# Two residual blocks on one core: the gate and the second mixer read their input turned without its norm

## The reference, cut to what matters

```
x = x + mix @ w_out
gate = sigmoid(rms_norm(x, g1) @ w_ple_gate + b);  x = x + gate * e
proj = rmsnorm(x, g2) @ w_in_2
xr, q, ckv, qi, ki, wi, gr, ga = split(proj)
y_rnn = rg_lru(causal_conv(xr), ...)            # 16 blocks of 128 columns
ckv = rmsnorm(ckv, g3);  ki = layernorm(ki)
y_attn = attention(q, ckv, relu(qi . ki) * wi, ...)   # 16 heads
x = x + (sigmoid(gr) * y_rnn + sigmoid(ga) * y_attn) @ w_o
x = x + peer(rmsnorm(x, g4), ...)
rms_norm(x, g) = x * rsqrt(mean(x * x) + eps) * g
```

## Time and profile before

| | |
|---|---|
| runs | 2815.0, 2816.63, 2817.1 us; median 2816.63 |
| profiled execution | 2815.1 us, span 2813.3 us |
| busy: PE, DVE, ACT, POOL | 2759.1, 1811.2, 1391.6, 257.1 us |
| DMA | 183 GB/s over the span |

### The profile page before, as it was taken

One profiled execution on the slowest core, in us unless ns is written; L12 is line 12 of the kernel. 1 busy time (PEld: TensorE's weight loads), 2 busy tenths in 40 slices (PEclk: granted clock), 3 DMA queues, 4 the chain that ended last, 5 costly groups with the idle time before them and its releaser, 6 DMA issues.

```text
span 2813.3 us, 49430 instructions
## 1 busy us (share of the span) xinstructions
PE 2759.1 (98%) x15452; PEld 2411.5 (86%) x15452; DVE 1811.2 (64%) x2894; ACT 1391.6 (49%) x2020; POOL 257.1 (9%) x342
## 2 busy tenths in 40 slices
PE   8999999899999999999999999999999999999998
PEld 6888877788888888889999999888888888888887
DVE  6666655657986666578886666666665555555555
ACT  5454545545565444455555554545554444444444
POOL 0000000000000000000004998000000000000000
PEclk9999999999999999999999999999999999999999
DMA  6544454464554444555565444666665556555574
GB/s 244 191 151 164 162 175 155 165 210 154 167 172 163 157 150 142 186 193 185 183 207 175 159 155 157 216 211 212 209 211 193 194 194 193 191 192 193 193 236 159
DMA packets 153551, 514.71 MB, mean 183 GB/s; under 512 B 17056, under 2 KB 33696, under 8 KB 152480
## 3 DMA queue, kind: packets, MB, share of 16 engines
q1 hardware_dynamic: 131904, 480.44, 52.0%
q10 hardware_dynamic: 21600, 33.70, 3.3%
HBM read 501.49 MB, written 12.58 MB: 183 GB/s over the span
## 4 chain that ended last, share of the span: by engine, by line
PE 59%; DVE 0%; ACT 0%; issue 0%; POOL 0%; DVEq 0%; ACTq 0%; POOLq 0%
PE bank L493 13%; PE bank L2111 8%; PE bank L2113 8%; PE bank L2112 8%; PE bank L498 6%; PE bank L478 3%; PE bank L479 3%; PE bank L480 3%; PE bank L2086 2%; PE bank L533 1%; PE bank L532 1%; PE bank L531 1%; PE bank L2061 0%; DVE act L1086 0%; PE bank L2131 0%
## 5 line engine op out<-in xcount | busy, mean ns | idle before, releaser
L455 DVE TENSOR_TENSOR w_lo<-raw,w_hi 128x1024 fp32r<-128x1024 f32 x904 | 1097.8, 1225 | 816.3 <-ACT w_hi L446 808.9
L446 ACT ACTIVATE w_hi<-raw 128x1024 fp32r<-128x1024 f32 x904 | 953.2, 1059 | 1027.5 <-PE bank L2113 369.3
L493 PE MATMUL bank<-act,w_hi 128*128 128x512 f32 x3072 | 787.9, 398 | 2.7 <-ACT w_hi L446 1.3
L493 PEld LDWEIGHTS bank<-act,w_hi 128*128 128x128 f32 x3072 | 554.1, 189 | 109.3 <-issue 6.2
L498 PEld LDWEIGHTS bank<-act,w_lo 128*128 128x128 f32 x3072 | 419.1, 190 | 31.2
L498 PE MATMUL bank<-act,w_lo 128*128 128x256 f32 x3072 | 428.1, 282 | 0.0
L2111 PE MATMUL bank<-w_hi,expert_act 128*128 128x512 f32 x1008 | 392.3, 389 | 0.1
L2112 PE MATMUL bank<-w_lo,expert_act 128*128 128x512 f32 x1008 | 392.2, 389 | 0.0
L2113 PE MATMUL bank<-w_hi,expert_act 128*128 128x512 f32 x1008 | 392.1, 389 | 0.0
L478 PE MATMUL bank<-act,w_hi 128*128 128x256 f32 x912 | 261.0, 286 | 3.3 <-DVE w_lo L455 2.7
L479 PE MATMUL bank<-act,w_hi 128*128 128x256 f32 x912 | 258.7, 284 | 0.0
(11 more groups left out here) (286 smaller groups left out, 2380.2 us busy)
## 6 DMA issues: line engine op xcount, KB each, us to landing
raw<-in_stream SPq DMA_DIRECT2D x904, 512.0 KB, 4.2
big<-in_ukv ACTq DMA_DIRECT2D x16, 512.0 KB, 5.2
z_kept<-cst ACTq DMA_DIRECT2D x64, 128.0 KB, 3.2
cst<-z_kept ACTq DMA_DIRECT2D x64, 128.0 KB, 3.9
big<-in_x SPq DMA_DIRECT2D x2, 1024.0 KB, 9.6
big<-in_rows ACTq DMA_DIRECT2D x2, 1024.0 KB, 8.8
big<-in_rg_w ACTq DMA_DIRECT2D x1, 2048.0 KB, 8.2
x_kept<-big ACTq DMA_DIRECT2D x1, 2048.0 KB, 6.6
```

The source lines that it names most:

```text
L446: act.activation(w_hi[:, s, :], raw[:, s, :], ACT.Copy).then_inc(hi_ready, 1)
L455: dve.tensor_tensor(w_lo[:, s, :], raw[:, s, :], w_hi[:, s, :].bitcast(F32), ALU.subtract).then_inc(lo_ready, 1)
L493: pe.matmul(bank[:, :], w_hi[:, s, kk * P:(kk + 1) * P], act2[:, k, :, :].rearrange("p a n -> p (a n)"), start=(k == 0), stop=False)
```

## The change

X itself is transposed, 512 columns at a time (`turn_block`, 8 transposes), in the middle of a later block of products: the first three blocks of w_out's output within w_out, the fourth within the first block of gate, and so on into ckv. The tiles for gate go to a buffer of their own (`gate_in_hi`, `gate_in_lo`). High and low parts are kept four tiles at a time behind the second split of a block. The factor of each token is applied to the results: in the bias addition of gate, in the copies of ckv, ki and wi, in the relu of the index scores, in the mask addition of the logits; xr, gr and ga, which have tokens along the row, are multiplied on GpSimd by a row of the factors. TensorE makes that row from ones and a diagonal matrix, and ScalarE keeps it. The last turn, ahead of the experts, stays as it was, as does the first. On VectorE, XP's addition moves ahead of the gates of the block before, and the softplus moves by one split; the fetch of the rnn table RGW moves behind ckv's splits. Some semaphores are merged (`row_ready`, `table_ready`), with the counts that go with it.

The diff, cut ("..." marks what is left out):

```diff
@@ -596,13 +607,20 @@
             with pool.Fori(0, KT) as j:
-                pool.wait_ge(rgw_ready, 16)
+                wait_summed(pool, block_of("rnn", j, 2, 0))
+                pool.wait_ge(row_kept, 1)
+                pool.tensor_tensor(XP[:, 3:3 + S], XP[:, 3:3 + S], RSTD_ROW, ALU.mult).then_inc(scaled, 1)
+                pool.wait_ge(table_ready, 16)
...
             with pool.Fori(0, H2) as h:
...
+                for n in range(2):
+                    wait_summed(pool, block_of("heads", h, 2, n))
+                    gate_rows = [TG, TA][n]
+                    pool.tensor_tensor(gate_rows, gate_rows, RSTD_ROW, ALU.mult).then_inc(scaled, 1)
@@ -652,6 +670,15 @@
+            def keep_hi_tiles(n, gain, high, b):
+                for pair in range(2):
+                    act.wait_ge(turned, n * KT + 4 * b + 2 * pair + 2)
+                    for kk in range(2):
+                        k = 4 * b + 2 * pair + kk
+                        act.activation(high[:, k, :], banks[4 + 2 * (b % 2) + pair][:, kk * S:(kk + 1) * S], ACT.Copy,
+                                       scale=gain[:, k:k + 1]).then_inc(act_hi_ready, 1)
@@ -750,21 +777,24 @@
             def split_and_square(part, base, i):
                 for k in range(16):
-                    if k == 15:
+                    if k == 15 and part == "w_o":
...
-                    if part == "w_out" and k == 5:
+                    if part == "w_out" and k == 6:
...
                     if k >= 4 and k % 4 == 1:
+                        if part == "w_out":
+                            keep_hi_tiles(1, pa("gate_gain"), gate_in_hi, k // 4 - 1)
...
-            keep_hi(1, pa("gate_gain"))
+            warm_root()
+            block_squares(added, 0, 3)
@@ -772,29 +802,34 @@
                         for t in range(TT):
...
-                    if 4 * b + k < 15:
-                        ahead(split_hi, act, "gate", 0, 8, 4 * b + k)
-                    if b and k == 1:
+                    ahead(split_hi, act, "gate", 0, 8, 4 * b + k)
+                    if k == 1 and not b:
+                        keep_hi_tiles(1, pa("gate_gain"), gate_in_hi, 3)
+                        root_of_sums(2)
+                    elif k == 1:
+                        keep_hi_tiles(2, pa("mix_gain"), act_hi, b - 1)
...
-            root_of_sums(3)
-            ahead(split_hi, act, "gate", 0, 8, 15)
-            keep_hi(2, pa("mix_gain"))
-            act.dma_start(RGW, rg_w).then_inc(rgw_ready, 16)
             for k in range(4):
...
+                if k == 1:
+                    keep_hi_tiles(2, pa("mix_gain"), act_hi, 3)
+                    root_of_sums(3)
+            act.dma_start(RGW, rg_w).then_inc(table_ready, 16)
+            act.wait_ge(rstd_ready, 4)
...
             for t in range(TT):
-                act.activation(CKV[:, t, :], banks[t][:, :], ACT.Copy).then_inc(ckv_kept, 1)
+                act.activation(CKV[:, t, :], banks[t][:, :], ACT.Copy, scale=rstd[:, t:t + 1]).then_inc(ckv_kept, 1)
...
             for t in range(TT):
@@ -814,11 +849,15 @@
                 for b in range(2):
-                    act.activation(REL[:, 2 * b:2 * b + 2, :].rearrange("p a n -> p (a n)"), banks[4 + b][:, :],
-                                   ACT.Relu, scale=ID ** -0.5).then_inc(rel_ready, 1)
+                    for t in range(TT):
+                        relu = act.activation(REL[:, 2 * b + t, :], banks[4 + b][:, t * S:(t + 1) * S], ACT.Relu,
+                                              scale=index_scale[:, t:t + 1])
+                    relu.then_inc(rel_ready, 1)
             for n in range(2):
...
+            act.wait_ge(row_made, 1)
+            act.activation(RSTD_ROW, banks[5][:, 0:S], ACT.Copy).then_inc(row_kept, 1)
@@ -887,8 +926,6 @@
-                wait_summed(act, block_of("heads", h, 2, 0))
-                act.activation(TG, TG, ACT.Tanh, scale=0.5).then_inc(gr_tanh, 1)
...
                 for t in range(TT):
...
+                act.wait_ge(scaled, H2 + h * 2 + 1)
+                act.activation(TG, TG, ACT.Tanh, scale=0.5).then_inc(gr_tanh, 1)
...
-                wait_summed(act, block_of("heads", h, 2, 1))
+                act.wait_ge(scaled, H2 + h * 2 + 2)
@@ -1092,8 +1131,19 @@
-                step(dve.reciprocal(rstd_ap, std_ap))
-                step.wait()
+                dve.reciprocal(rstd_ap, std_ap).then_inc(rstd_ready, 1)
+                dve.wait_ge(rstd_ready, i + 1 + i // 4)
+            def keep_lo_tiles(i, gain, high, low, b):
+                for pair in range(2):
+                    dve.wait_ge(act_hi_ready, i * KT + 4 * b + 2 * pair + 2)
+                    for kk in range(2):
+                        k = 4 * b + 2 * pair + kk
+                        dve.scalar_tensor_tensor(out=low[:, k, :],
+                                                 in0=banks[4 + 2 * (b % 2) + pair][:, kk * S:(kk + 1) * S],
+                                                 scalar=gain[:, k:k + 1], in1=high[:, k, :].bitcast(F32),
+                                                 op0=ALU.mult, op1=ALU.subtract).then_inc(act_lo_ready, 1)
@@ -1340,34 +1390,37 @@
                     for k in range(3):
...
-                        if part == "w_out" and (b, k) == (1, 1):
+                        if part == "w_out" and b and k == 1:
+                            keep_lo_tiles(2, pa("gate_gain"), gate_in_hi, gate_in_lo, b - 1)
+                        if part == "w_out" and (b, k) == (1, 2):
...
                     for t in range(TT):
...
-                    if b < 3:
+                    if b < 3 or part == "w_out":
...
             for n in range(2):
...
-            normed_rows(2)
-            keep_lo(2, pa("gate_gain"))
-            ahead(split_lo, dve, "w_out", 0, 8, 15)
...
                 for k in range(3):
...
+                    if k == 1 and not b:
+                        keep_lo_tiles(2, pa("gate_gain"), gate_in_hi, gate_in_lo, 3)
+                        norm_rows(2)
+                    elif k == 1:
+                        keep_lo_tiles(3, pa("mix_gain"), act_hi, act_lo, b - 1)
...
                 for t in range(TT):
-                    dve.tensor_tensor(SC_G[t], banks[2 * n + t][:, :], gate_row[:, cols], ALU.add)\
-                       .then_inc(gate_pre, 1)
-                if b < 3:
-                    ahead(split_lo, dve, "gate", 0, 8, 4 * b + 3)
+                    dve.scalar_tensor_tensor(out=SC_G[t], in0=banks[2 * n + t][:, :], scalar=rstd[:, t:t + 1],
+                                             in1=gate_row[:, cols], op0=ALU.mult, op1=ALU.add).then_inc(gate_pre, 1)
+                ahead(split_lo, dve, "gate", 0, 8, 4 * b + 3)
@@ -1379,13 +1432,19 @@
             for n in range(2):
...
-            normed_rows(3)
-            keep_lo(3, pa("mix_gain"))
-            ahead(split_lo, dve, "gate", 0, 8, 15)
+            step(dve.memset(ONES, 1.0))
             for k in range(4):
...
+                if k == 1:
+                    keep_lo_tiles(3, pa("mix_gain"), act_hi, act_lo, 3)
+                    norm_rows(3)
+                    step(dve.tensor_scalar(index_scale, rstd, ID ** -0.5, None, ALU.mult))
+                    step(dve.tensor_scalar(logit_scale, rstd, P ** -0.5, None, ALU.mult))
+                    for t in range(TT):
+                        step(dve.tensor_scalar(RSTD_DIAG[:, t, :], ident, rstd[:, t:t + 1], None, ALU.mult))
+                    step.wait()
+                    dve.sem_inc(rstd_ready, 1)
@@ -1483,11 +1542,12 @@
             def rnn_block(j, first=False):
                 if not first:
...
+                add_halves(dve, XP[:, 3:3 + S], banks[0], block_of("rnn", j, 2, 0))
+                if not first:
...
-                add_halves(dve, XP[:, 3:3 + S], banks[0], block_of("rnn", j, 2, 0))
-                wait_summed(dve, block_of("rnn", j, 2, 0))
+                dve.wait_ge(scaled, j + 1)
...
-                    step(dve.scalar_tensor_tensor(out=LG.rearrange("p t n -> p (t n)"), in0=banks[4][:, :],
-                                                  scalar=float(P) ** -0.5, in1=AMASK, op0=ALU.mult, op1=ALU.add))
+                    for t in range(TT):
+                        step(dve.scalar_tensor_tensor(out=LG[:, t, :], in0=banks[4][:, t * S:(t + 1) * S],
+                                                      scalar=logit_scale[:, t:t + 1],
+                                                      in1=AMASK[:, t * S:(t + 1) * S], op0=ALU.mult, op1=ALU.add))
@@ -1790,6 +1852,16 @@
+            def turn_block(turn, b, taken):
+                pe.wait_ge(taken[b % 2], b // 2 * 2 + 3)
+                if 4 * turn + b >= 2:
+                    pe.wait_ge(act_lo_ready, 2 * KT + 4 * (4 * turn + b - 1))
+                for k in range(4 * b, 4 * b + 4):
+                    for t in range(TT):
+                        off = (k % 2) * S + t * P
+                        ins = pe.transpose(banks[4 + 2 * (b % 2) + k % 4 // 2][:, off:off + P],
```

(43 more changed lines are left out.)

47 lines of the change are left out of this document (30 added, 17 removed).

## The result

| | before | after |
|---|---|---|
| median of 4 runs | 2815.82 us | 2792.14 us (2791.59 to 2795.2) |
| span of the profiled execution | 2813.3 us | 2790.4 us |
| ratio of the runs | | 0.992, 95% interval 0.9908 to 0.9933 |

What follows compares the result with a forecast made beforehand. TensorE, busy 98% of the span, was taken as the bound. Gains of 17.7 (turns), 1.2 (rnn) and 2.0 (first head) less 0.9 (last head) made 20.0 us: 2796.6 us forecast, range 2792.5 to 2804.0.

Steps and rivals of the forecast that it cites:

- The turns: Around gate: 25.11 us without products, less 7.0 for 64 transposes, 0.3 for switches, 0.1 for softplus, gives 17.7 us.
- The tightest place: In ckv, splits and low tiles end about T + 16.8, wanted at T + 17.2 (T: gate products' end); cost nothing.
- The holes of 25.11 us: TensorE's stretches without a product before gate (11.34 us) and before ckv (13.77 us), each containing 32 transposes.
- rnn: Rnn stage: the earlier addition frees bank 0 sooner, but TensorE gains only 1.2 us, with ends 3.4 and below zero.
- VectorE's work per block is the same, and the next bound is close: In rnn: bank 1's addition ends at 781.97, TensorE wants it at 783.25, so TensorE comes forward only 1.2 us.
- First head: ScalarE takes the root 2.2 us earlier, so TensorE's waits of 1.26 and 0.74 us go: 2.0 us gained.
- Last head: No cover for GpSimd's multiplication: TensorE's 1.18 us wait for the kept probabilities grows by 0.9 us.
- rival 3: The 2 MB table fetch holds the loads of qi: 6 us more, 2802.6 us; chance 0.05.
- (1): VectorE and GpSimd lock each other, 0.7 us in each of 8 rnn blocks: about 2802 us; chance 0.14.
- (2): The turns hide worse, a 0.5 us stall at each of 8 places of transposes: 2800.6 us; chance 0.10.
- (5): The change does nothing, transposes waiting for something as late as before: 2816.6 us; chance 0.02.
- (4): Slower: waiting for GpSimd's product bounds the rnn loop once past its 3.6 us cover; 2835 us at 6 us; chance 0.03.

Runs made afterwards that it cites:

- experiment 6: The changed kernel with every transpose in the blocks issued twice, 64 more: 2800.21 us, ratio 0.9949 to the kernel before.
- Experiment 7: The changed kernel with the last group of 8 transposes after two units of ckv, not four: 2796.83 us, ratio 0.9937.
- experiment 9: The kernel before with its two turns transposing X without the norm factor, transposes still in one lump: 2806.03 us, ratio 0.9967.
- experiment 2: The kernel before with only the rnn addition into XP moved ahead of the gates: 2809.43 us, ratio 0.9982.
- experiment 4: The kernel before with GpSimd's rnn gate-weight copy also waiting for the end of VectorE's first split: 2813.21 us, ratio 0.9992.
- experiment 5: The kernel before with ScalarE's tanh of gr behind the root and exponentials in the first head alone: 2814.34 us, ratio 0.9995.
- experiment 8: The changed kernel with GpSimd's rnn multiplication made four times, 2795.97 us (ratio 0.9935), and eight times, 2841.82 us (1.0096).
- experiment 1: The changed kernel with the rnn addition into XP back behind the gates and second split: 2803.86 us, ratio 0.9963.

## Why the prediction was right, and where its size was off

**The turns** (17.7, measured 17.9). Right in each step: 0.109 us a transpose (experiment 6), and 0.05 us for a group's switches, 0.4 us in all, where I took 0.3; the 0.1 us for the softplus did not show as a wait. The tightest place held: the low tiles in ckv ended at T + 16.5 us where I had T + 16.8 (T = 543.8, VectorE's row below), and TensorE started on them without a wait. Experiment 7 shows that the margin of 2.8 us at the gating was real.

```profile
550.46 1.29 DVE L1431 SCALAR_TENSOR_TENSOR big<-big 128x512 f32<-128x512 f32 x2
...
554.11 4.63 DVE L466 TENSOR_TENSOR w_lo<-raw,w_hi 128x1024 fp32r<-128x1024 f32 x4 [2.02 <-ACT w_hi L457]
558.65 1.66 DVE L1143 SCALAR_TENSOR_TENSOR act<-bank,par,act 128x256 fp32r<-128x256 f32 x4
```

The holes of 25.11 us were counted as time without a product, so all that stood in them was in the sum, VectorE's late low tiles too, which experiment 9 found and which no step had named, and TensorE's half clock in the lumps, which the prediction did not see: its price of 0.109 us holds for the transposes' new place, not for their old one.

**rnn** (1.2, measured 3.56): the term that was mis-sized. The failed step is "VectorE's work per block is the same, and the next bound is close". The addition of bank 1 was the next bound, as said: in the changed kernel it ends at 761.80 and TensorE starts on that bank at 762.01. But it came 2.4 us earlier than I had it, since VectorE's cycle shrank from 12.37 to 12.12 us. Half of the 0.25 us is the dependent start behind the addition, 0.45 us where the gates now start after 0.33 (experiments 2 and 4); the other half is GpSimd's copy, which stretched the split from 1.22 to 1.35 us in just the six blocks with a period of 12.37 us. That the chain addition, product, gate matmul, copy held the copy 0.13 us ahead of the split there is my reading of the two rows; that keeping it off the split is worth 0.96 us is measured. The 1.35 us stood in the earlier trace rows; I took it for VectorE's own work. A cycle of 12.12 us is still a little over TensorE's 12.06, but over eight blocks it adds up to only 0.5 us, and TensorE waits nowhere in rnn.

**First head** (2.0, measured 2.66). The root behind the tanh was 2.15 us by itself (experiment 5). The rest is 0.4 us ahead of the logits, which the new rnn order brings (experiment 2), and 0.1 us of unknown cause.

**Last head** (-0.9, measured -1.02): as forecast, 0.8 us and a semaphore. **Nothing elsewhere**: GpSimd's product in the 14 steady heads, the four relus, the split logits and the 2 MB table moved nothing in the traces; the period of a head is 16.87 us in both. The place of the 2 MB fetch was not tried by itself; rival 3 falls since TensorE's wait at the start of qi is 2.7 us in both traces and no new one comes in.

**The rivals.** (1) did not come, though the lock is real: the product lies beside the one-input reciprocal (experiment 8). (2) and (5) are excluded by the groups' 22.68 us. (4) needs a product that outlasts its cover of 3.45 us, over five times the 0.64 us that it takes. The row of 0.8 us that it leaned on (line 616, 842 ns) is of 128x128, half the product's size and not a quarter. The range ran 4.1 us below the forecast: 2.2 for the rnn term's upper end of 3.4 us and 1.9 for the rest. The traces' gain of 22.9 us lies inside it (2793.7). What took the time below it is the medians, whose difference of 23.7 us is 0.8 above that of the traces, and the base, which was 0.8 us lower than in the prediction. The first of these is not explained by any run.

One thing that differs from trace to trace: in both traces TensorE runs at half clock for 3.2 us behind the 2.7 us wait that opens qi. In six of the seven other traces of the changed kernel's variants it doesn't, and TensorE is 1.4 us earlier from 591 us on. What decides it isn't shown. The changed kernel's:

```profile
576.51 0.33 PE L491 MATMUL bank<-act,w_lo 128*128 128x256 f32 x1
576.64 0.41 PE L489 MATMUL bank<-act,w_hi 128*128 128x256 f32 x1
576.85 0.42 PE L490 MATMUL bank<-act,w_hi 128*128 128x256 f32 x1
```

The pace goes from 0.12 to 0.21 us a product at 576.64 (granted 0.57 over 576 to 580). The same happens behind the 2.0 us wait of the last head: full clock in the changed kernel, but a granted clock of 0.5 for 3.4 us and 1.6 us lost in the traces of experiments 1, 6, 7 and of the one with four multiplications. Differences of one or two microseconds between two runs' times are of this kind, and none of the terms above rests on them.

## What to carry to other kernels

A factor per token commutes with a product, so a norm need not stand between two matrix stages; half of what that brought here was not waiting for the factor, the other half that the transposes could then lie among products, where they cost only their own 0.109 us each. When an engine sets the pace, read its cycle for instructions that are longer there than elsewhere (1.35 against 1.22 us) and for starts that wait on the instruction just ahead: a move that frees the other engine can take those away too, so the next bound must be worked out with a shorter cycle as its other end. Work given to GpSimd is free only inside its cover and beside one-input instructions of VectorE: find both before choosing its place.

## What was not expected of the hardware

- A wait of 2.6 us in the middle of products cost 4.3 us: the products behind it ran at 1.2 GHz for 3 us (experiment 7). Behind the 2.0 us wait of the last head the pace was full at once in the changed kernel, and in four variants it was half for 3.4 us and cost 1.6 us more, so even a wait of 2 us can cost nearly twice its length.
- Which of GpSimd and VectorE pays for an overlap turns on a quarter of a microsecond: a copy that begins 0.13 us ahead of a split lengthens the split by 0.13 us; one that begins 0.12 us inside it, or 0.3 us inside it (experiment 2), is itself stretched from 0.40 to 1.36 or 1.16 us, and the split not at all.
- Eight transposes of 128x128 follow each other 0.109 us apart at full clock, and the products behind them start within 0.3 us. A lump of 32 behind a wait of 4.6 us started them 0.21 us apart, at half clock, until the clock rose among the transposes themselves (460.2).
